# Fetching expert weights in 2 MB transfers, one TensorE wait for two ring places

## The reference

```python
logits = tok @ w_router + b_router          # 32 experts
top_val, top_idx = lax.top_k(logits, 4); gate = softmax(top_val)
# for each expert e, on the tokens that chose it:
hid = xb @ w_e_in[e] + b_e_in[e]            # 1024 x 2048, 8 MB
act = min(glu, 7) * sigmoid(1.702 * glu) * (clip(lin, -7, 7) + 1)
y   = act @ w_e_out[e] + b_e_out[e]         # 1024 x 1024, 4 MB
```

## Time and profile before

| | us |
|---|---|
| median of 3 runs | 1311.4 (1308.96 to 1313.85) |
| the profiled execution | 1309.35 |
| its span, first to last instruction | 1307.6 |
| TensorE busy | 1047.7 (80%) |
| VectorE busy | 499.5 (38%) |
| ScalarE busy | 177.5 (14%) |

### The profile page before, as it was taken

The page is one execution under the profiler, slowest core; times in us unless marked ns, Lnnn a source line. Parts: engine busy times, 40 slices in busy tenths (PEclk is TensorE's granted clock), DMA queues, the critical chain, the costliest instruction groups (busy, mean ns, idle before and its releaser), DMA issues.

```text
span 1307.6 us, 31581 instructions
## 1 busy us (share of the span) xinstructions
PE 1047.7 (80%) x12600; PEld 478.3 (37%) x12601; DVE 499.5 (38%) x1147; ACT 177.5 (14%) x510; POOL 52.9 (4%) x120
## 2 busy tenths in 40 slices
PE   3799897499998779779789969996978997787940
PEld 2556554243442324224334424442433442332310
DVE  0294446734442323223333433442323342241428
ACT  0101432411111101001111101110111110110100
POOL 2800000000000000000000000000000000000013
PEclk9799998599998888979889989998988997897975
DMA  9986765369999999997998996299799899999980
GB/s 324 332 300 248 250 239 223 134 246 420 420 421 420 419 420 422 420 421 318 420 420 331 421 420 271 80 421 422 323 421 420 333 421 420 420 420 421 420 326 36
DMA packets 78171, 457.15 MB, mean 350 GB/s; under 512 B 9163, under 2 KB 16245, under 8 KB 28865
## 3 DMA queue, kind: packets, MB, share of 16 engines
q1 hardware_dynamic: 73600, 450.18, 85.1%
q10 hardware_dynamic: 4481, 5.59, 1.3%
HBM read 452.51 MB, written 3.79 MB: 349 GB/s over the span
## 4 chain that ended last, share of the span: by engine, by line
PE 36%; DMA 23%; SPq 22%; DVE 10%; issue 5%; DVEq 2%; ACT 1%; ACTq 0%; POOL 0%
PE bank L1636 15%; DMA w<-in_w_e_out 14%; SPq L401 9%; SPq L404 7%; DMA w<-in_w_e_in 6%; PE bank L1665 6%; PE bank L1616 3%; SPq L382 2%; PE comb L1595 2%; DMA mt<-in_ln_b 2%; PE bank L1514 1%; SPq L368 1%; DMA w<-in_w_ada 1%; PE bank L1629 1%; DVE mt L1232 1%
## 5 line engine op out<-in xcount | busy, mean ns | idle before, releaser
L1636 PE MATMUL bank<-w,mt 128*32 128x512 f32 x3264 | 393.4, 625 | 50.6 <-DMA w<-in_w_e_in 50.5
L1189 DVE TENSOR_TENSOR xy<-comb,xy 128x1024 f32<-128x1024 f32 x156 | 185.2, 1215 | 238.7 <-PE comb L1595 238.7
L1665 PE MATMUL bank<-w,mt 128*32 128x256 f32 x3264 | 201.0, 394 | 38.2 <-DMA w<-in_w_e_out 25.1
L1636 PEld LDWEIGHTS bank<-w,mt 128*32 128x32 f32 x3264 | 96.3, 113 | 307.3 <-issue 210.6
L1228 DVE TENSOR_SCALAR mt<-bank 128x256 f32<-128x256 f32 x51 | 21.7, 425 | 391.7 <-PE bank L1636 391.7
L1665 PEld LDWEIGHTS bank<-w,mt 128*32 128x32 f32 x3264 | 100.9, 113 | 122.6 <-DMA w<-in_w_e_out 38.5
L1616 PE MATMUL bank<-pick,hb 128*128 128x32 bf16 x2448 | 79.3, 179 | 56.1 <-issue 39.3
L1595 PE MATMUL comb<-mt,gpickT 32*128 32x256 f32 (+1 forms) x1248 | 116.3, 457 | 2.0 <-DVE xy L1189 1.4
L1616 PEld LDWEIGHTS bank<-pick,hb 128*128 128x128 bf16 x2448 | 75.0, 97 | 79.3 <-issue 79.3
L807 ACT ACTIVATE mt<-mt 128x256 f32<-128x256 f32 x51 | 21.2, 417 | 502.2 <-DVE mt L1228 502.2
L1617 PE MATMUL bank<-pick,hb 96*128 96x32 bf16 x408 | 72.5, 179 | 0.0
(11 more groups left out here) (313 smaller groups left out, 766.3 us busy)
## 6 DMA issues: line engine op xcount, KB each, us to landing
w<-in_w_e_in SPq DMA_DIRECT2D x256, 1024.0 KB, 26.1
w<-in_w_e_out SPq DMA_DIRECT2D x128, 1024.0 KB, 21.9
w<-in_w_ada SPq DMA_DIRECT2D x12, 2048.0 KB, 11.2
w<-in_w_in SPq DMA_DIRECT2D x3, 2048.0 KB, 22.0
w<-in_w_in SPq DMA_DIRECT2D x2, 1024.0 KB, 21.5
w<-in_w_out SPq DMA_DIRECT2D x4, 512.0 KB, 9.9
w<-in_w_out SPq DMA_DIRECT2D x2, 1024.0 KB, 12.5
w<-mod_rows SPq DMA_DIRECT2D x4, 512.0 KB, 6.4
```

The costliest lines, as they stand in the source:

```text
L1189: return v.tensor_tensor(rows, comb[0:TS[t], :, c:c + 256], rows, ALU.add)
L1636: ins = mm(quarter(bank[0][SLOTS * q:SLOTS * (q + 1), :], 0), xT[:, SLOTS * k:SLOTS * (k + 1)], quarter(slot[s], q), start=False, stop=(k ...
L1665: ins = mm(bank[7][SLOTS * q:SLOTS * (q + 1), 0:256], hid, slot[s][:, D * (k % 2) + 256 * q:D * (k % 2) + 256 * (q + 1)], start=False, sto ...
```

## The change

Two neighbouring chunks are fetched by one transfer of 2 MB into two neighbouring places of the ring, and only the semaphore of the first of the two is raised and waited for. Since 12 j, the chunk's number and 20 are even, a pair never runs over the ring's end. Where the loads stand in the order of SP, what SP waits for, the bytes, the places and the matmuls are as before.

```diff
             def load(e, j, first, last):
-                for c in range(first, last):
+                for c in range(first, last, 2):
                     s = slot_of(j, c)
+                    dst = W[:, 2 * D * s:2 * D * (s + 2)].rearrange("p (k n) -> p k n", k=2)
                     if c < DK:
-                        src = weights(w_e_in, e)[P * c:P * (c + 1), :]
-                        sp.dma_start(slot[s], src).then_inc(ld_slot[s], 16)
+                        src = weights(w_e_in, e)[P * c:P * (c + 2), :].rearrange("(k p) n -> p k n", p=P)
                     else:
-                        src = weights(w_e_out, e)[2 * P * (c - DK):2 * P * (c - DK + 1), :].rearrange("(p k) n -> p (k n)", k=2)
-                        sp.dma_start(slot[s], src).then_inc(ld_slot[s], 16)
+                        src = weights(w_e_out, e)[2 * P * (c - DK):2 * P * (c - DK + 2), :].rearrange("(k p m) n -> p k (m n)", p=P, m=2)
+                    sp.dma_start(dst, src).then_inc(ld_slot[s], 16)
...
-                        pe.wait_ge(ld_slot[s], turns[turn_of(j, k)])
+                        if k % 2 == 0:
+                            pe.wait_ge(ld_slot[s], turns[turn_of(j, k)])
...
                     for k in range(DK):
                         s = slot_of(j, DK + k // 2)
-                        if k % 2 == 0:
+                        if k % 4 == 0:
                             pe.wait_ge(ld_slot[s], turns[turn_of(j, DK + k // 2)])
```

## The result

| | before | after |
|---|---|---|
| median, us (11 runs each) | 1310.0 (1308.96 to 1313.85) | 1316.15 (1314.51 to 1320.36) |
| profiled execution, us | 1309.35 | 1319.8 |
| its span, us | 1307.6 | 1318.0 |
| mean granted clock | 0.898 | 0.913 |

The changed kernel takes 1.0048 times as long, with a 95% interval of 1.0034 to 1.0063: some 6 us slower, just under the 0.5% that was called no change, though the interval reaches past it. One execution of the kernel before, beside e2, e4, e7 and e8 further down, took 2428.7 us where the others lie between 1307 and 1315 us; it counts as slow, and the ratios leave it out.

What follows compares the result with a forecast made beforehand. Transfers at 420 GB/s and TensorE alone were taken to alternate on the path. The terms 6.6 - 2.5 + 0.2 = +4.3 us gave a median of 1315.7 us against 1311.4 us, range 1307.5 to 1323 us.

Steps and rivals of the forecast that it cites:

- What bounds the kernel: Expert stage: weight transfers at 420 GB/s alternate with TensorE alone, changing hands five times ahead of stretches without transfers.
- The last pair: At five hand-overs from transfers to TensorE, one extra chunk of work after the last landing: +6.6 us (4.0 to 9.7).
- the forecast case: The prediction's main case, +4.3 us on the execution and a median of 1315.7 us; chance 0.65.
- The first of a pair: In stretches paced by transfers, TensorE sees a pair's first chunk up to 2.50 us later; cost nothing.
- Completions: Semaphore raises at transfer ends: 192 fewer at 13 ns each, 2.5 us less (0 to 11.7).
- Issue: SP's first issue at each of five transfer restarts takes 0.04 us more: +0.2 us (0 to 1.6).
- A (the clock): Rival: longer pauses drop TensorE's clock to half at all five hand-overs, +13.2 us, 1324.6 us; chance 0.15 (three or more).
- B: Rival: each transfer's completion costs an engine the whole 61 ns, so -4.9 us, 1306.5 us; chance 0.09.
- C: Rival: later TensorE lets the queue empty, a sixth stretch without transfers lacking 7 us, 1322.7 us; chance 0.05.
- D: Rival: each 2 MB transfer is carried out as two with as many completions, 1318.2 us; chance 0.06.

Runs made afterwards that it cites:

- e2: Changed kernel, but chunks 10 and 11 of each expert fetched and waited for one by one; 1310.3 us, 0.9999 of the kernel before.
- e4: Kernel before with transfers of 4 MB into four places and one wait for each four chunks; 1326.9 us, ratio 1.0129.
- e7: Kernel before, with TensorE releasing places after chunk 1 so chunks 8 and 9 of the next expert go earlier; 1302.6 us, ratio 0.9944.
- e8: Kernel before, with TensorE releasing a place after chunk 0 so chunk 8 of the next expert goes earlier; 1297.3 us, ratio 0.9903.
- n0: Kernel before, with only block numbers held at 1 or more by a register operation, an edit all follow-up kernels share; 1311.4 us, ratio 0.9999.
- a0: Changed kernel (pairs), with only block numbers held at 1 or more by a register operation; 1317.5 us, 1.0043 of the kernel before.
- e1: Kernel before, still with 1 MB transfers, but TensorE waits for both chunks of a pair ahead of the first; 1316.6 us, ratio 1.0042.
- e3: Kernel before, with only the wait for chunk 11 moved ahead of chunk 10; 1320.4 us, ratio 1.0071.
- e5: Kernel before, with each expert's last chunk fetched in two transfers of 0.5 MB, each with its own wait; 1314.4 us, ratio 1.0020.

## Why the prediction was right, and where its terms were off

The forecast was 1315.7 us and +4.3 us on the execution; the median is 1316.15 us, and the pieces behind the head are +5.7 us (0.2, 5.2, 0.0 and 0.2 before rounding).

**What bounds the kernel** was read rightly. Five hand-overs, five dry stretches, transfers and blocks unchanged within 0.2 us; e7 and e8 confirm the other side of each dry stretch.

**The last pair**, +6.6 us forecast: +5.2 us measured, 5.1 between n0 and a0. With every hand-over at full clock in both kernels it would be 5 x 0.87 = 4.3 us; the rest is the clock. A full-clock hand-over grew from 3.41 to 4.28 us, by 0.87, where 0.92 was forecast. At the one of L1636, costed at 1.94 us for a slow clock, it was 6.46 - 3.74 = 2.7 us: before, TensorE was behind when the last chunk landed (at 690.39 us) and did not wait for it, and the slow clock was just ending (0.50 up to 689 us, 0.86 from 689 to 692 us); with pairs TensorE waited for the last pair at L1666 and worked it off at half clock, 3.64 us. The one that was slow in the earlier trace rows (915.47 us) came out at full clock and cost nothing, 4.28 instead of 4.36 us, where 1.94 us had been forecast. That is the difference: the forecast case took each hand-over's clock as fixed, and it is not.

**The first of a pair** costs nothing, as said: the window of 288 us is at 421 GB/s, and e2, which keeps ten of twelve chunks in pairs, is at 0.9999.

**Completions**, -2.5 us forecast: this is the term that was mis-sized. Within the stretches that the transfers pace, landings are 2.485 us apart for 1 MB and 4.969 us for 2 MB, so a pair saves 0.001 us, some 0.1 us over the five stretches. n0, a0 and e1 have 608.1, 608.9 and 608.9 us of transfer: the pairs of a0 are not below the two with 384 completions. The 13 ns came from taking the small-packet queue's 61 ns apart; what is left there after the bytes is then no price of these transfers' completions. The trace has those as packets of their own in the weights' queue, 4 bytes and 9.6 ns each, 7040 of them before and 3968 after. For the 192 that each engine is spared that would be 1.8 us, if they held up the bytes; the landings' spacing shows that they do not. The prediction's end of the range, that the windows show the engines fully busy at 420 GB/s whatever is in them, was the right value.

**Issue**, +0.2 us forecast, is inside the 0.2 us that the transfers grew and can't be told from nothing.

**The sum.** +6.6 was 1.4 us too much and -2.5 was 2.5 us too much the other way, so that the two errors hid part of each other, which is luck; the total came out 1.4 us low (5.7 against 4.3). Part of the closeness of 1315.7 to 1316.15 is also luck of the base: the median of before was 1311.4 us in 3 runs and is 1310.0 in 11, and from that base the change costs 6.1 us rather than 4.8.

**The rivals.** A (the clock) did not decide here: one of five at half clock, mean granted clock 0.913 where it was 0.898 before. Its price was set too high as well: 5.29 + 1.94 = 7.2 us for a paired hand-over at half clock, where the longest measured are 6.5 us (after, e1). The rule cited with it from the Trainium skill (TensorE: Matmul & The Clock Gate, HAM oscillation), that waits between short bursts let the clock fall, is borne out in part: e3 shows it at every hand-over, the kernels with a wait for each pair at one (after) and two (a0, e1) of five. B fell with the landings' spacing, C with the count of dry stretches, D with the 3072 packets that are gone. The other page that was cited (DMA: Bandwidth & Descriptors, Measured), by which a larger transfer runs faster, is not borne out in this busy queue: 420, 421 and 421 GB/s in the same window at 1, 2 and 4 MB, and 421 GB/s at 1 MB in e7.

## What to carry to other kernels

Where transfers and an engine take turns on the path, what counts is the work that stands behind the last wait, not the number of waits or transfers: make the last step before a hand-over small, and merge only those ahead of it (e2 keeps five sixths of the bytes merged at no cost). There is an end to it: one chunk of 1 MB was the best last step here, and its halves cost more in transfer than they saved on TensorE (e5). Look at both ends of a hand-over: releasing the first place of a ring as soon as it is free, instead of four together, was worth 1%, more than twice what the pairs cost. Where windows showed the engines fully busy at 420 GB/s with 1 MB transfers, larger ones gained nothing.

## What the runs showed of the hardware

- In a busy queue a transfer's own cost is not measurable between 1 and 4 MB: landings are 2.485 us apart at 1 MB, 4.969 us at 2 MB and 9.943 us at 4 MB. With 0.5 MB for each expert's last two transfers, in rows of 4 KB, the five stretches took 5.6 us more, 4.2 us of it in the first 13 us behind the restarts.
- Some transfers land late. In each profile but e4's, eight to ten landings come 0.6 to 1.7 us after their turn (3.8 instead of 2.485 us, say), some 12 us in all in n0, as much as e8 gained. One of them is the first, second or third transfer of `w_e_in` behind each of the five restarts in n0, and the others are at like places in most kernels, whatever the waits. In before and n0 each of the 19 lands 2.1 to 4.2 us after the start of a 16 KB packet of the queue that the page lists as "instruction" (78 packets, some 1.07 us long each); but most of those packets have no late landing behind them, so the cause is not shown.
- The granted clock at a hand-over is not a function of the pause ahead of it alone. 1.41 and 1.42 us of pause, and 2.94 us twice in the changed kernel, stand ahead of both levels; 2.8 to 4.0 us in e3 ahead of the lower one alone. What decides it stays open.
